# Decoder step in fp32: the high part of each weight block is rounded on ScalarE, the low part is subtracted on GpSimd over the raw block, and TensorE's projection loops are unrolled

## The reference, cut to what matters

```python
def squared_relu_mlp(x, w_up, w_down):
    h = jax.nn.relu(x @ w_up)
    return (h * h) @ w_down
...
z = zxbcdt[..., :SSD_D_INNER]
xbc = zxbcdt[..., SSD_D_INNER:SSD_D_INNER + SSD_CONV_DIM]
```

## Time and profile before

| what | us |
|---|---|
| median of 3 timed runs | 1894.43 |
| the runs | 1891.1, 1894.95, 1894.43 |
| span of the profiled execution (first to last instruction) | 1891.5 |
| busy TensorE matmul / VectorE / ScalarE / GpSimd | 1580.9 / 1284.9 / 444.8 / 1324.6 |
| mean granted TensorE clock | 0.911 |

### The profile page before, as it was taken

How to read it: one execution, slowest core, us unless ns; L and a number is a source line. 1 busy time by engine, 2 the same in 40 slices (tenths; PEclk the granted TensorE clock), 3 DMA queues, 4 the chain that set the end, 5 groups by cost and what they waited for, 6 DMA issues and landing times.

```text
span 1891.5 us, 29700 instructions
## 1 busy us (share of the span) xinstructions
PE 1580.9 (84%) x11978; PEld 1480.8 (78%) x11978; DVE 1284.9 (68%) x1123; ACT 444.8 (24%) x1085; POOL 1324.6 (70%) x586
## 2 busy tenths in 40 slices
PE   5898734887749969999999679996678699999995
PEld 5898623687748969999999579983338699999995
DVE  7999824889994179603865665798883698028745
ACT  3212201245562122100210211114553321002100
POOL 5767522775666878888888667664425789888886
PEclk8999866998869979999999789996889799999998
DMA  8222895024442313333332214261321123223331
GB/s 144 79 69 76 15 4 12 6 86 165 163 150 60 97 45 89 89 92 96 90 89 89 67 56 134 68 212 68 112 68 45 56 87 91 89 89 91 98 89 45
DMA packets 93048, 159.40 MB, mean 84 GB/s; under 512 B 54179, under 2 KB 54563, under 8 KB 92707
## 3 DMA queue, kind: packets, MB, share of 16 engines
q1 hardware_dynamic: 92962, 158.25, 35.8%
HBM read 142.07 MB, written 16.16 MB: 84 GB/s over the span
## 4 chain that ended last, share of the span: by engine, by line
PE 54%; DVE 33%; issue 6%; another core or an unknown queue 3%; ACT 2%; POOL 2%; DMA 1%; SPq 0%; DVEq 0%; POOLq 0%; ACTq 0%
PE GP L492 16%; PE GP L494 16%; PE GP L493 16%; DVE cacc L1265 3%; DVE hT L1367 2%; DVE acc L1387 2%; DVE hc L1327 2%; DVE hs L1324 1%; DVE kq L1464 1%; DVE hs L1321 1%; DVE aL L1362 1%; DVE misc L1508 1%; DVE cacc L1263 1%; DVE yss L1328 1%
## 5 line engine op out<-in xcount | busy, mean ns | idle before, releaser
L402 POOL TENSOR_TENSOR wH<-wraw,cst 128x1024 fp32r<-128x1024 f32 x216 | 532.3, 2465 | 334.8 <-PE GP L494 324.5
L492 PE MATMUL GP<-aH,wH 128*128 128x260 f32 x1920 | 559.1, 291 | 102.5 <-DVE aL L1362 35.6
L406 POOL TENSOR_TENSOR wL<-wraw,wH 128x1024 fp32r<-128x1024 f32 x216 | 573.2, 2654 | 16.9
L494 PE MATMUL GP<-aH,wL 128*128 128x260 f32 x1920 | 551.7, 287 | 0.0
L493 PE MATMUL GP<-aL,wH 128*128 128x260 f32 x1920 | 551.1, 287 | 0.0
L492 PEld LDWEIGHTS GP<-aH,wH 128*128 128x128 f32 x1920 | 371.5, 194 | 112.6 <-issue 62.2
L492 PE MATMUL GP<-hidH,wH 128*128 128x260 f32 x1536 | 440.9, 287 | 7.8 <-DVE hidL L1338 7.3
L494 PE MATMUL GP<-hidH,wL 128*128 128x260 f32 x1536 | 436.1, 284 | 0.0
L493 PE MATMUL GP<-hidL,wH 128*128 128x260 f32 x1536 | 435.0, 283 | 0.0
L493 PEld LDWEIGHTS GP<-aL,wH 128*128 128x128 f32 x1920 | 372.1, 194 | 0.1
L494 PEld LDWEIGHTS GP<-aH,wL 128*128 128x128 f32 x1920 | 371.7, 194 | 0.0
(11 more groups left out here) (252 smaller groups left out, 2027.5 us busy)
## 6 DMA issues: line engine op xcount, KB each, us to landing
wraw<-wblk SPq DMA_DIRECT2D x216, 512.0 KB, 3.6
hs<-ssm_in SPq DMA_DIRECT2D x16, 512.0 KB, 3.8
sssm<-hs SPq DMA_DIRECT2D x16, 512.0 KB, 2.8
ktile<-kcache SPq DMA_DIRECT2D x16, 512.0 KB, 3.6
vtile<-vcache SPq DMA_DIRECT2D x16, 512.0 KB, 4.1
hT<-x_t SPq DMA_DIRECT2D x4, 520.0 KB, 5.2
kt_out<-kT SPq DMA_DIRECT2D x1, 2080.0 KB, 6.3
vt_out<-vT SPq DMA_DIRECT2D x1, 2080.0 KB, 10.1
```

Of the source, the lines that this page charges most:

```text
L402: pool.tensor_tensor(wH[:, d, :].rearrange("p (k n) -> p k n", k=8), raw[:, s, :].rearrange("p (k n) -> p k n", k=8), cst[:, C_ONE:C_ONE + ...
L406: pool.tensor_tensor(wL[:, d, :], raw[:, s, :], wH[:, d, :].bitcast(F32), ALU.subtract).then_inc(w_lo, 1)
L492: pe.matmul(out, lh, rh, start=first, stop=False)
L494: return pe.matmul(out, ll, rh, start=False, stop=last)
```

## The change

The high part moves to ScalarE as an activation Copy with fp32r output, in 3 slots (HIS = 3). The low part stays on GpSimd, and is written over the raw block, of which there are now 5 slots (RAW = 5). So SP may load block j only when TensorE has used block j-5. The instructions on ScalarE are placed by hand: after the PSUM reads of a tile, up to the block three after the one that TensorE has just used. All hardware loops around the projections become straight code on SP, GpSimd and TensorE. The multiply by ones and GpSimd's wait for TensorE are gone.

```diff
-RAW, SPL = 4, 2
+RAW, HIS = 5, 3
-    O_RAW, O_SPL, O_SM = 166400, 182784, 199168
+    O_RAW, O_HI, O_SM = 166400, 186880, 199168
-    wH = at("wH", [P, SPL, 1024], O_SPL, F32R)
-    wL = at("wL", [P, SPL, 1024], O_SPL + SPL * 4096, F32R)
+    wH = at("wH", [P, HIS, 1024], O_HI, F32R)
+    wL = at("wL", [P, RAW, 1024], O_RAW, F32R)
...
         def stream(a, b):
-            with sp.Fori(a // RAW, b // RAW) as i:
-                for s in range(RAW):
-                    sp.wait_ge(w_lo, i * RAW + (s + 1 - RAW))
-                    sp.dma_start(raw[:, s, :], wblk[bass.ds(i * RAW + s, 1), :, :].rearrange("o p n -> p (o n)")
-                                 ).then_inc(raw_in[s], 16)
+            for j in range(a, b):
+                sp.wait_ge(blk, j - RAW + 1)
+                sp.dma_start(raw[:, j % RAW, :], wblk[j, :, :]).then_inc(raw_in[j % RAW], 16)
...
         for m in range(NPAIR):
-            b = zb + m
-            sp.wait_ge(w_lo, b + 1 - RAW)
-            sp.dma_start(raw[:, b % RAW, :], wblk[b, :, :]).then_inc(raw_in[b % RAW], 16)
             sp.wait_ge(hs_new, m + 1)
...
+            stream(zb + m, zb + m + 1)
-        stream(zb + NPAIR, kb)
+        stream(zb + NPAIR, qb_)
...
     @block.gpsimd
-            pool.tensor_tensor(wH[:, d, :].rearrange("p (k n) -> p k n", k=8),
-                               raw[:, s, :].rearrange("p (k n) -> p k n", k=8),
-                               cst[:, C_ONE:C_ONE + 1, :].broadcast_to([P, 8, P]), ALU.mult).then_inc(w_hi, 1)
-            pool.wait_ge(w_hi, i * RAW + (s + 1))
-            pool.tensor_tensor(wL[:, d, :], raw[:, s, :], wH[:, d, :].bitcast(F32), ALU.subtract).then_inc(w_lo, 1)
+        def lows(n):
+            nonlocal low
+            for j in range(low, n):
+                pool.wait_ge(w_hi, j + 1)
+                pool.tensor_tensor(wL[:, j % RAW, :], raw[:, j % RAW, :], wH[:, j % HIS, :].bitcast(F32), ALU.subtract
+                                   ).then_inc(w_lo, 1)
+            low = max(low, n)
-        stream(SPL, BLOCK0["z"])
+        lows(BLOCK0["z"] + HIS)
...
     @block.scalar
+        def highs(n):
+            nonlocal high
+            for j in range(high, min(n, NBLK)):
+                sc.wait_ge(raw_in[j % RAW], 16 * (j // RAW + 1))
+                if j >= HIS:
+                    sc.wait_ge(blk, j - HIS + 1)
+                A(wH[:, j % HIS, :], raw[:, j % RAW, :], ACT.Copy).then_inc(w_hi, 1)
+            high = max(high, min(n, NBLK))
...
             A(xs4[:, m, :, 3], G[g + 1][:, SEQ - HALF:HALF], ACT.Copy).then_inc(taken, 1)
+            highs(m + 1 + HIS)
...
             A(zs[:, m % 2, HV[1]], G[gb + 1][:, 0:HALF], ACT.Silu).then_inc(taken, 1)
+            highs(BLOCK0["z"] + m + 1 + HIS)
...
                 if own_f:
+                    done = BLOCK0[nm] + BLOCKS[nm] * (m + 1)
+                    highs(done + HIS - 1)
...
                 else:
+                    done = BLOCK0[f"down{p // 2}b"] + 2 * (m + 1)
+                    highs(done + HIS)
...
                     A(rel[:, m % 2, HV[1]], G[gb + 1][:, 0:HALF], ACT.Relu).then_inc(taken, 1)
+                    highs(BLOCK0[name] + m + 1 + HIS)
...
                 hidden_hi(32 * l + 16 * v + 15, 15)
+                if v == 0:
+                    highs(BLOCK0[f"up{l}b"] + HIS)
```

More of the change, by code:

```diff
@@ L315, in stream @@
         def stream(a, b):
-            with sp.Fori(a // RAW, b // RAW) as i:
-                for s in range(RAW):
-                    sp.wait_ge(w_lo, i * RAW + (s + 1 - RAW))
-                    sp.dma_start(raw[:, s, :], wblk[bass.ds(i * RAW + s, 1), :, :].rearrange("o p n -> p (o n)")
-                                 ).then_inc(raw_in[s], 16)
-        zb, kb, ob = BLOCK0["z"] + RAW, BLOCK0["q"] + RAW, BLOCK0["o"] + RAW
+            for j in range(a, b):
+                sp.wait_ge(blk, j - RAW + 1)
+                sp.dma_start(raw[:, j % RAW, :], wblk[j, :, :]).then_inc(raw_in[j % RAW], 16)
+        zb, qb_, kb, ob = (BLOCK0[n] + RAW for n in ("z", "q", "k", "o"))
         stream(RAW, zb)
@@ L358, in _ @@
         vb = BLOCK0["v"]
-        stream(kb, vb)
+        stream(qb_, kb)
         sp.wait_ge(blk, BLOCK0["k"])
@@ L395, in _ @@
     def _(pool):
[L396 to L400, removed]
-            pool.tensor_tensor(wH[:, d, :].rearrange("p (k n) -> p k n", k=8),
-                               raw[:, s, :].rearrange("p (k n) -> p k n", k=8),
-                               cst[:, C_ONE:C_ONE + 1, :].broadcast_to([P, 8, P]), ALU.mult).then_inc(w_hi, 1)
-            pool.wait_ge(w_hi, i * RAW + (s + 1))
-            pool.tensor_tensor(wL[:, d, :], raw[:, s, :], wH[:, d, :].bitcast(F32), ALU.subtract).then_inc(w_lo, 1)
[L408 to L423, removed]
+        low = 0
+        def lows(n):
[5 more added lines that the diff above has]
+            low = max(low, n)
         def scale_output(p):
@@ L459, in _ @@
                 masked_adt(k)
-        at_ = BLOCK0["z"]
-        stream(at_, BLOCK0["out"] + SPL)
-        at_ = BLOCK0["out"] + SPL
+        lows(BLOCK0["out"] + HIS)
         for q in range(NPAIR):
@@ L494, in three, with tile @@
             return pe.matmul(out, ll, rh, start=False, stop=last)
[L496 to L501, removed]
+        def tile(name, m, inH, inL, each_k=None):
+            nk, t, b = BLOCKS[name], TILE0[name] + m, BLOCK0[name] + m * BLOCKS[name]
+            if t >= 2:
+                pe.wait_ge(taken, t - 1)
             for kb in range(nk):
-                d = (b[1] + kb) % SPL
-                pe.wait_ge(w_lo, b[0] + kb + 1)
+                hi, lo = (b + kb) % HIS, (b + kb) % RAW
+                pe.wait_ge(w_lo, b + kb + 1)
@@ L505, in tile @@
                 for k in range(8):
+                    kk = kb * 8 + k
                     if each_k is not None:
[L507 removed]
+                        each_k(kk)
                     for h in range(2):
[L509 to L511 removed]
+                        o_ = G[2 * (t % 2) + h][:, 0:HALF]
+                        lh, ll = wH[:, hi, k * P:(k + 1) * P], wL[:, lo, k * P:(k + 1) * P]
@@ L512, in tile @@
                         ins = three(o_, lh, ll, inH[:, kk, HV[h]], inL[:, kk, HV[h]],
-                                    kb == 0 and k == 0, kb == nk - 1 and k == 7)
+                                    kk == 0, kb == nk - 1 and k == 7)
                 ins.then_inc(blk, 1)
         def gemm(name, inH, inL, after=None, each_k=None, tiles=None, inside=None):
[L518 to L522, removed]
@@ L524, in gemm @@
-            if after is not None:
-                for m in range(n):
-                    one(m, each_k if m == 0 else inside and (lambda k, m=m: inside(m, k)))
-                    after(m)
-                return
-            a, e = tiles or (0, n)
-            if a == 0:
-                one(0, each_k)
-                one(1)
-                a = 2
-            with pe.Fori(a // 2, e // 2) as i:
-                for u in range(2):
-                    tile(name, (i * 2 + (m0 + u), (m0 + u) % 2), (i * (2 * nk) + (b0 + u * nk), b0 + u * nk),
-                         inH, inL, True)
+            a, e = tiles or (0, dict((g, n) for g, n, _ in GEMMS)[name])
@@ L540, in _ @@
+            for m in range(a, e):
+                tile(name, m, inH, inL, each_k if m == 0 else inside and (lambda k, m=m: inside(m, k)))
+                if after is not None:
+                    after(m)
         pe.wait_ge(in_one, 16)
@@ L895, in _ @@
             A(sq8[:, t, :], hT[:, t, :], ACT.Square).then_inc(sq0, 1)
+        highs(2)
         sc.wait_ge(mm0, 1)
```

20 lines of the change are left out of this document (11 added, 9 removed).

## The result

The changed kernel takes 1795.24 us (median of 4 runs, 1791.8 to 1799.17) against 1894.62 us for the kernel before (median of 4 runs beside it). The ratio is 0.9476 with a 95% interval of 0.9455 to 0.9498. The profiled execution of the changed kernel has a span of 1793.7 us and a time of 1795.44 us.

A forecast was written before the change was run, and what follows sets the result against it. TensorE bounds the MLP, and VectorE, slowed by GpSimd, bounds xbc and z. Stage gains sum to 66 us, taking the 1891.5 us span to 1825.5; with 2.9 us from span to median, 1828 us, range 1800 to 1860.

The forecast's parts named there:

- The bound: In xbc and z VectorE leads, slowed by GpSimd: about 2.0 us per GpSimd instruction in xbc, 1.75 in z.
- Start and xbc: Input scalings meet fewer GpSimd instructions, 2.5 us; in xbc TensorE leads again and its xs waits go, 22 us.
- Scan: From xbc's end to z: the state-write stall moves but keeps its length; GpSimd's z parts leave scan's end, 3.5 us.
- z: 16 fewer GpSimd instructions free 28 us of VectorE; 20 us kept, since three close engines would wait on each other.
- Boundaries, MLP, out, o: Last sums of squares at three stage ends, 3 us; where TensorE is full, its waits for GpSimd go, 2 us.
- q: Before q, TensorE's 9.4 us wait for VectorE's sum goes, and the half clock after it: 10 us.
- v: The first query's 3.5 us wait for qz, behind two rotary products at contended length, shrinks: 3 us.
- Attention: The attention stage was left at no gain in the forecast's sum.
- Unrolling at nothing: Turning the projection loops into straight code neither gains nor costs time: 0 us.
- rival of instruction supply: Straight code in place of loops stalls instruction supply: 1913 us at 0.5 us a block, 1964 at 0.8; chance 0.05.
- ScalarE's copy: ScalarE's new 128x1024 high-part copy takes 1.1 us, 238 us in sum, with 6.8 us of slack a block.
- More: Rival: all lost VectorE time in z returns, attention and v gain a few; 80 to 90 us, 1808 us; chance 0.14.

The follow-up runs named there:

- the packed kernel: The kernel after, with the samples' convolution rows first packed by one ScalarE copy before their transfer: 1746.8 us, ratio to before 0.923.

## Why the forecast fell short, and what held

- **The bound.** "VectorE's slowness is GpSimd's activity": shown. With the multiply put back and ScalarE's copy kept, the gain is gone (1.0001). It holds for the instructions that the forecast looked at, not for reductions (1.22 us in all 16) or the copies out of PSUM. The Trainium skill, page "Advanced Engine Details and Errata", section "Mode Summary", says that the second Vector SBUF port is shared with GpSimd and that GpSimd's instructions and VectorE's in two-port mode block each other. That the port is the cause here is not shown: no run tells which mode an instruction was in. The runs show only that GpSimd slows VectorE and that a second ScalarE copy does not.
- **Start and xbc**, 24.5 forecast, 28.6 measured. The multiply put back costs 21.4 us in xbc and 4.6 at the start. TensorE leads again, as said; the start, at 2.5, was too small (its 8 scalings take 7.49 us, where the forecast had 8.8).
- **Scan**, 3.5 forecast, 1.4 measured; but the stretch varies by itself, 194.6 to 198.5 us in kernels with the code of after in it and 199.9 to 202.3 with that of before. The former are all shorter, by 1.4 to 7.8 us: the term's sign is borne out, its size is not settled. The stall moved whole and kept its length, 57.2 for 55.1 us.
- **z is the step that failed.** "Three engines so close will make each other wait, so I keep 20": z with its tail gave 38.6 us. The forecast's rows gave 16 x 1.75 = 28, and no row showed a wait among the three engines that would take 8 of it. What the runs showed in its place: the multiply put back costs 1.77 us for each tile between z.2 and z.15 (115.15 less 92.17 us, 13 tiles), so the rate was right and the discount was not. A tile took 7.1 us, not 7.6. TensorE's granted clock was 0.98 in these tiles instead of 0.87, and its busy time fell from 7.1 to 6.8 us a tile. VectorE was busy 6.9 us a tile instead of the forecast's 7.6: 1.0 us over its 5.85 alone, where the forecast gave the subtraction left 1.9. That reductions go on beside GpSimd fits this; it was not tried. Even ScalarE at 127 of 130 us took nothing. The other part of the miss is that the term had nothing past z.15. The tail to out.0, where VectorE gates the last tile, gained 3.8 us and lost 5.6 in the run with the multiply back in z. And 5.1 us from out.0 to out.2 came from block 43's parts leaving VectorE's way; the forecast looked for moved steps of GpSimd in the scan, but not here.
- **Boundaries, MLP, out, o**, 5 forecast, 8.4 measured; the mean of the squares' sum went from 2.01 (L1354) to 1.44 us (L1325).
- **q**, 10 forecast, 11.9 measured, of which 6.9 come back with the multiply. **v**, 3 forecast, 1.2 measured: the wait for qz, which was to go, is still 2.3 of its 3.5 us.
- **Attention**, left at nothing, gave 7.8. The forecast gave no reason for the nothing. 3.4 us are at the entry, where VectorE is less behind at v's end. The other 4.4 follow from where the page instructions fall and are luck: the next change may take them back, as in the packed kernel (154.7 us there, 150.1 after).
- **Unrolling at nothing**: shown, 1.0004. The rival of instruction supply is dead: the instruction queue moves 95 packets instead of 56 and the MLP block stays at 5.74 us. (That rival counted some 170 blocks leaving the loops; on TensorE they are 150, which makes its 0.39 us a block 0.44.)
- **ScalarE's copy**, estimated 1.1 us, is 1.061; its slack was real.
- Of the rivals, "More" (1808, chance 0.14) named the right places, all of z and a few in attention, and was still 13 us short: it had nothing for z's tail and little for attention. Its own 80 to 90 us end at 1804, and the range ended at 1800 for that. The measured z in place of 20 gives 1809, attention 1802, and the small terms, mostly xbc, the boundaries and the MLP, the rest.

## What to carry to other kernels

Where GpSimd and VectorE work side by side, price a GpSimd instruction by up to its own length on VectorE (1.0 to 2.2 us of 2.5 here), less where VectorE reduces or reads PSUM, and take it off wherever VectorE leads. In this kernel ScalarE was the better place even when it was nearly full. Take the row's rate for a term and follow the stage to the point where the next one no longer depends on it, its tail included, rather than discount for what might come. Then look for short VectorE steps in a dependent chain beside GpSimd (here attention, 34 to 39 us) and for transfers in pieces of a few bytes that stand ahead of others in a queue (57 us): both were larger than they looked, and neither showed up as a busy engine.

## What was not expected of the hardware

- A VectorE copy of 3 columns takes 0.16 us, and 2.38 us when it meets a GpSimd instruction. The added time was 2.0 to 2.2 us for the copy, a multiply-add of 512 columns (0.55 to 2.65) and three fused ones (2.33 to 4.33), so small steps suffer most.
- VectorE's reductions of 128x1024 took 1.22 us in all 16 cases before and after, 9 of them beside GpSimd, and its copies of 128x260 out of PSUM 0.43 us with GpSimd beside them or not.
- GpSimd is slowed too, by less: GpSimd's subtraction of 1024 columns had a mean of 2654 ns beside the busier VectorE of before and 2495 ns after.
- A transfer of 288 KB in pieces of 12 bytes takes 93.6 to 95.6 us and holds back the transfers behind it; the same bytes in rows of 2304 take 2.2 us, for one ScalarE copy.
- ScalarE busy 98% of a stretch (127.01 of 130 us) did not lengthen it.
